# Adding the experts' rows in memory by the scatter, with their gates applied before it

## The reference, cut to what matters

```
logits = xt @ w_router + b_router
top_val, top_idx = lax.top_k(logits, 4)
gate = softmax(top_val)
for each expert e, for the tokens that chose it (rows xb):
    hb = xb @ w_e1[e] + b_e1[e]                 # (1024, 2048)
    y_rows = clamped_swiglu(hb) @ w_e2[e] + b_e2[e]   # (1024, 1024)
y = zeros(T, D).at[row_tok].add(y_rows * row_gate[:, None])
h = layer_norm(DEEPNORM_ALPHA * h + y, ln2_g, ln2_b)
```

## Time and profile before

| | |
|---|---|
| median of 3 runs | 1656.25 us (1654.56 to 1658.57) |
| the profiled execution | 1654.45 us, its span 1652.7 us |
| busy in the span | TensorE 91%, VectorE 29%, ScalarE 15%, POOL 14% |
| chain that ended last | PE 69%, DMA 19% |
| queue q1 (issued by SP) | 445.10 MB, 68.4% of 16 engines' span |
| mean granted clock of TensorE | 0.979 of full |

### The profile page before, as it was taken

The page is one execution under the profiler, slowest core; times in us unless marked ns, Lnnn a source line. Parts: engine busy times, 40 slices in busy tenths (PEclk is TensorE's granted clock), DMA queues, the critical chain, the costliest instruction groups (busy, mean ns, idle before and its releaser), DMA issues.

```text
span 1652.7 us, 30470 instructions
## 1 busy us (share of the span) xinstructions
PE 1498.5 (91%) x12438; PEld 687.6 (42%) x12439; DVE 483.3 (29%) x933; ACT 249.9 (15%) x302; POOL 232.7 (14%) x301
## 2 busy tenths in 40 slices
PE   7999999999999878999997888998799999999955
PEld 6744444444445623344343333333334333344322
DVE  5034343200005634223232223223223222232226
ACT  4011232100001121111110111101011010010112
POOL 1060000000000001211211211211211121111225
PEclk9999999999999889999999999999999999999987
DMA  5523100153304479999999999999999999999945
GB/s 187 181 77 91 30 1 0 48 187 89 89 2 202 153 313 416 413 416 417 415 415 416 415 414 417 416 414 417 415 414 416 417 415 414 387 367 395 411 161 213
DMA packets 136151, 474.31 MB, mean 287 GB/s; under 512 B 16700, under 2 KB 62500, under 8 KB 102840
## 3 DMA queue, kind: packets, MB, share of 16 engines
q1 hardware_dynamic: 123264, 445.10, 68.4%
q0 software_dynamic: 10896, 16.83, 2.8%
q10 hardware_dynamic: 1960, 11.94, 1.8%
HBM read 470.12 MB, written 20.97 MB: 297 GB/s over the span
## 4 chain that ended last, share of the span: by engine, by line
PE 69%; DMA 19%; DVE 3%; issue 3%; SPq 3%; ACT 1%; POOL 1%; ACTq 0%; POOLq 0%; DVEq 0%
PE ps L1417 22%; DMA big<-in_w_e 16%; PE ps L1445 13%; PE ps L1285 7%; PE ps L1206 5%; PE ps L1315 3%; PE ps L1343 3%; PE ps L1299 3%; PE ps L1167 3%; SPq L457 2%; PE ps L1293 2%; DMA rest<-x_rows,idx 2%; PE ps L1234 1%; PE ps L1410 1%; PE ps L1513 1%
## 5 line engine op out<-in xcount | busy, mean ns | idle before, releaser
L1417 PE MATMUL ps<-big,rest 128*32 128x512 f32 x5120 | 571.9, 599 | 70.0 <-DMA big<-in_w_e 36.6
L1417 PEld LDWEIGHTS ps<-big,rest 128*32 128x32 f32 x5120 | 162.0, 111 | 443.2 <-issue 443.1
L1445 PE MATMUL ps<-big,rest 128*32 128x256 f32 x5120 | 287.4, 381 | 19.6 <-DMA big<-in_w_e 16.5
L1445 PEld LDWEIGHTS ps<-big,rest 128*32 128x32 f32 x5120 | 166.8, 110 | 130.8 <-issue 34.9
L1076 DVE TENSOR_TENSOR rest<-ps,rest 128x1024 f32<-128x1024 f32 x32 | 39.2, 1224 | 602.4 <-PE ps L1417 602.4
L736 ACT ACTIVATE rest<-ps 128x1024 f32<-128x1024 f32 x33 | 68.6, 2080 | 459.3 <-PE ps L1410 459.3
L569 POOL DMA_INDIRECT expert_rows<-rest,slot x128 | 127.3, 995 | 59.5 <-issue 32.9
L565 POOL COPY slot<-P 128x4 uint32 x32 | 5.9, 184 | 742.1 <-DVE rest L1095 742.1
L740 ACT ACTIVATE rest<-ps 128x1024 f32<-128x1024 f32 x32 | 32.8, 1024 | 410.1 <-PE ps L1438 410.1
L1206 PE MATMUL ps<-big,rest 128*128 128x512 f32 x192 | 82.8, 592 | 2.8 <-ACT big L612 2.8
L1095 DVE TENSOR_TENSOR rest<-ps,rest 128x1024 f32<-128x1024 f32 x32 | 39.2, 1224 | 132.2 <-PE ps L1445 132.2
(11 more groups left out here) (213 smaller groups left out, 1145.2 us busy)
## 6 DMA issues: line engine op xcount, KB each, us to landing
big<-in_w_e SPq DMA_DIRECT2D x384, 1024.0 KB, 19.8
rest<-in_w_in SPq DMA_DIRECT2D x14, 1024.0 KB, 5.2
big<-expert_rows ACTq DMA_DIRECT2D x4, 2048.0 KB, 15.7
gate_area<-in_w_in SPq DMA_DIRECT2D x8, 512.0 KB, 5.4
rest<-in_w_in SPq DMA_DIRECT2D x8, 512.0 KB, 4.7
big<-in_w_out SPq DMA_DIRECT2D x1, 4096.0 KB, 13.0
X<-in_x SPq DMA_DIRECT2D x4, 512.0 KB, 9.6
gate_area<-in_w_branch_mlstm SPq DMA_DIRECT2D x4, 512.0 KB, 6.4
```

Of the source, the lines that this page charges most:

```text
L1417: last = mm(ps[TB * g:TB * (g + 1), b, :], xT[:, k, b, :], W1[:, k, HW_ * g:HW_ * (g + 1)], start=(k == 0), stop=(k == KD - 1))
L1445: last = mm(ps[TB * g:TB * (g + 1), 4 + b // 2, YW * (b % 2):YW * (b % 2 + 1)], aT[:, b, k % 2, TB * (k // 2):TB * (k // 2 + 1)], W2[:, k ...
```

## The change

- `y_dram`, with a row for each choice, is replaced by `sum_dram`, with a row for each token. Slot numbers become token numbers. The scatter gets `compute_op=ALU.add`: the piece is added to what stands in memory.
- `sum_dram` begins as `DEEP_ALPHA` times the first norm's rows: ScalarE scales `X0` tile by tile and stores it, ahead of the softmax's exponential. POOL waits for these stores (`sum_started`) before its loop.
- The gates are put into the same places as the slots by 16 products, ahead of the second pair of weight rows of the first round, and spread by four, ahead of its last pair. VectorE makes 16 one-hots for them instead of the 16 diagonals, and copies the results out.
- `take_y` gets a second instruction: `yS` times the gates, before `y_ready`.
- At the end four loads of 512 KB bring the sums into `X0`. VectorE takes statistics and subtracts the mean, ScalarE computes the root and multiplies the tile before by it, VectorE adds the bias; the last tile is scaled and biased by VectorE alone. ScalarE's table for logarithm and exponential is loaded ahead of it. TensorE and POOL have nothing left to do there.

```diff
-    y_dram = nc.dram_tensor("expert_rows", (S, TOPK, D), F32, kind="Internal").ap()
-    y_quarters = y_dram.rearrange("t k (g n) -> (t k g) n", g=CG)
+    sum_dram = nc.dram_tensor("sum_rows", (S, D), F32, kind="Internal").ap()
+    sum_quarters = sum_dram.rearrange("t (g n) -> (t g) n", g=CG)
...
                 for b in range(NB):
-                    pool.indirect_dma_start(out=y_quarters, out_offset=bass.IndirectOffsetOnAxis(ap=slot[:, b:b + 1], axis=0),
+                    pool.indirect_dma_start(out=sum_quarters, out_offset=bass.IndirectOffsetOnAxis(ap=slot[:, b:b + 1], axis=0),
                                             in_=yS[:, b, :], in_offset=None,
-                                            bounds_check=S * TOPK * CG - 1, oob_is_err=False).then_inc(y_stored, 16)
+                                            bounds_check=S * CG - 1, oob_is_err=False, compute_op=ALU.add).then_inc(y_stored, 16)
...
             pool.wait_ge(tables_ready, 2)
+            pool.wait_ge(sum_started, 16 * NT)
...
+            act.wait_ge(x1_stored, 16 * NT)
+            for i in range(NT):
+                act.activation(X0v[:, i, :], X0v[:, i, :], ACT.Copy, scale=DEEP_ALPHA).then_inc(x1_scaled, 1)
+                act.wait_ge(x1_scaled, i + 1)
+                act.dma_start(sum_dram[P * i:P * (i + 1), :], X0v[:, i, :]).then_inc(sum_started, 16)
             act.wait_ge(dist_ready, 1)
...
             for i in range(NT):
-                act.dma_start(yg[:, i], y_dram[P * i:P * (i + 1)]).then_inc(yg_landed[i], 16)
+                act.dma_start(X0v[:, i, :], sum_dram[P * i:P * (i + 1), :]).then_inc(sum_landed[i], 16)
+            act.preload_act_table_set("natural_log_exp_and_others")
             for i in range(NT):
-                rstd(NORM2 + i)
+                s0 = 16 * i
+                act.wait_ge(var2_ready, i + 1)
+                step(act.activation(stat[:, s0 + 14:s0 + 15], stat[:, s0 + 13:s0 + 14], ACT.Ln))
+                act.activation(stat[:, s0 + 14:s0 + 15], stat[:, s0 + 14:s0 + 15], ACT.Exp, scale=-0.5).then_inc(rstd2_ready, 1)
+                if i >= 1:
+                    act.wait_ge(centred, i)
+                    act.activation(X0v[:, i - 1, :], X0v[:, i - 1, :], ACT.Copy, scale=stat[:, s0 - 2:s0 - 1]).then_inc(scaled, 1)
...
                 nc.vector.tensor_tensor(yS, ps[:, 4:6, :].rearrange("p a (b n) -> p (a b) n", n=YW),
-                                        b2_all.rearrange("p (a n) -> p a n", a=1).broadcast_to([P, NB, YW]), ALU.add).then_inc(y_ready, 1)
+                                        b2_all.rearrange("p (a n) -> p a n", a=1).broadcast_to([P, NB, YW]), ALU.add).then_inc(y_biased, 1)
+                dve.wait_ge(y_biased, it)
+                gates = gate_table[:, bass.ds(it * NB - NB, NB)].rearrange("p (b a) -> p b a", a=1)
+                nc.vector.tensor_tensor(yS, yS, gates.broadcast_to([P, NB, YW]), ALU.mult).then_inc(y_ready, 1)
...
-                nc.vector.tensor_scalar(gate_diag[:, n, :], ident[:], gw[:, i, k:k + 1], None, ALU.mult).then_inc(diags_ready, 1)
+                nc.vector.tensor_scalar(iter_oh[:, n, :], iota_row, itern[:, n:n + 1], gw[:, i, k:k + 1], ALU.is_equal, ALU.mult).then_inc(gate_oh_ready, 1)
+            dve.wait_ge(gates_done, 1)
+            nc.vector.tensor_copy(gates_f, ps[:, 4, 0:N_ITER]).then_inc(gates_read, 1)
+            dve.wait_ge(gates_spread, 1)
+            nc.vector.tensor_copy(gate_table.rearrange("p (n b) -> p b n", b=NB), ps[:, 5, :].rearrange("p (b n) -> p b n", b=NB)).then_inc(gate_table_ready, 1)
...
+            def gate_products():
+
+                pe.wait_ge(gate_oh_ready, TOPK * NT)
+                for n in range(TOPK * NT):
+                    last = mm(ps[:, 4, 0:N_ITER], place_oh[:, n, :], iter_oh[:, n, :], start=(n == 0), stop=(n == TOPK * NT - 1))
+                last.then_inc(gates_done, 1)
+
+            def gate_copies():
+
+                pe.wait_ge(gates_read, 1)
+                pe.wait_ge(tables_ready, 2)
+                for b in range(NB):
+                    last = mm(ps[:, 5, N_ITER * b:N_ITER * (b + 1)], sv[:, b, :], gates_f, start=True, stop=True)
+                last.then_inc(gates_spread, 1)
...
             for k0 in range(0, KD, 2):
+                if k0 == 2:
+                    gate_products()
+                if k0 == 6:
+                    gate_copies()
                 fc1_rows(1, first_blocks, k0)
```

More of the change, by code:

```diff
@@ L345, in build_program @@
         y_stored = sem("y_stored")
-        yg_landed = [sem(f"yg_landed{i}") for i in range(NT)]
+        sum_landed = [sem(f"sum_landed{i}") for i in range(NT)]
         ln2_landed = sem("ln2_landed")
@@ L581, in _ @@
             scatter(n_it)
-            pool.wait_ge(x1_scaled, 1)
-            pool.wait_ge(diags_ready, TOPK * NT)
-            for i in range(NT):
-                pool.wait_ge(yg_landed[i], 16)
-                row = yg[:, i, TOPK - 1, :]
-                step(nc.gpsimd.tensor_scalar(row, row, gatew[:, TOPK * i + TOPK - 1:TOPK * (i + 1)], None, ALU.mult))
-                nc.gpsimd.tensor_tensor(X0v[:, i, :], X0v[:, i, :], row, ALU.add).then_inc(fourth_added, 1)
         @block.scalar
@@ L1118, in _, with norm_2_statistics @@
             dve.wait_ge(ln2_landed, 32)
-            for i in range(NT):
-                t = X0v[:, i, :]
-                dve.wait_ge(fourth_added, i + 1)
-                for n in range(D // BANK):
-                    dve.wait_ge(combined, 2 * i + n + 1)
-                    half = t[:, BANK * n:BANK * (n + 1)]
-                    nc.vector.tensor_tensor(half, half, ps[:, 2 * (i % 2) + n, :], ALU.add).then_inc(combined_read, 1)
-                    dve.wait_ge(combined_read, 2 * i + n + 1)
-                    piece_statistics(NORM2 + i, n, half)
-                close_statistics(NORM2 + i, D // BANK)
+            def norm_2_statistics(i):
+                t = X0v[:, i, :]
+                s0 = 16 * i
+                dve.wait_ge(sum_landed[i], 16)
+                for n in range(D // BANK):
+                    piece_statistics(NORM2 + i, n, t[:, BANK * n:BANK * (n + 1)])
+                step(nc.vector.bn_aggr(stat[:, s0 + 12:s0 + 14], stat[:, s0:s0 + 12]))
+                nc.vector.tensor_scalar(stat[:, s0 + 13:s0 + 14], stat[:, s0 + 13:s0 + 14], LN_EPS, None, ALU.add).then_inc(var2_ready, 1)
+                layer_norm_center(NORM2 + i, t)
@@ L1129, in _, with norm_2_bias @@
+            def norm_2_bias(i):
+                dve.wait_ge(scaled, i + 1)
+                nc.vector.tensor_tensor(X0v[:, i, :], X0v[:, i, :], bias[:], ALU.add).then_inc(out_ready, 1)
+            for i in range(NT):
+                norm_2_statistics(i)
+                y = norm_2_root(i)
                 if i >= 1:
-                    layer_norm_scale(NORM2 + i - 1, X0v[:, i - 1, :], out_ready)
-                layer_norm_center(NORM2 + i, t)
-            layer_norm_scale(NORM2 + NT - 1, X0v[:, NT - 1, :], out_ready)
+                    norm_2_bias(i - 1)
@@ L1135, in _ @@
+            dve.wait_ge(centred, NT)
+            nc.vector.scalar_tensor_tensor(out=X0v[:, NT - 1, :], in0=X0v[:, NT - 1, :], scalar=y, in1=bias[:],
+                                           op0=ALU.mult, op1=ALU.add).then_inc(out_ready, 1)
         @block.tensor
```

47 lines of the change are left out of this document (26 added, 21 removed).

## The result

The changed kernel takes 1745.19 us (median of 5 runs, 1735.95 to 1750.11), the kernel before 1656.25 us (1654.56 to 1658.57). The ratio is 1.0532, with a 95% interval of 1.0497 to 1.0568. That is 89 us more, where 5 us more was predicted and 1688 us was the upper end. The profiled execution took 1735.95 us, with a span of 1734.2 us; it is the fastest of the five, so its trace shows some 9 us less of the loss than the median has.

A forecast was written before the change was run, and what follows sets the result against it. Weight loading was taken to bound the kernel up to 1277 us, then TensorE's products. First round 5.1, added read 13.3, gather lateness 5.3, minus tail 18.5 gave +5.2 us on 1656.25: 1661.5 us, range 1643 to 1688.

The forecast's parts named there:

- What bounds the kernel before: Expert rounds: weight landings decide up to 1277 us, then TensorE's products, broken twice by gathers of 8.4 us each.
- Tail: After the last bias addition: smaller loads and VectorE alone setting the pace gain 18.5 us (16.5 to 19.5).
- drain: Tail: the accumulating write takes longer to land before the sums can be loaded, 1 us (0 to 3).
- First round: TensorE's 20 extra matmuls placing and spreading the gates delay the first round: +5.1 us (2.5 to 10.4).
- The added read on the DMA engines: Rounds before 1277 us: reading old rows costs one more transfer of the same bytes, +13.3 us (0 to 26.6).
- The gathers' lateness: Last three rounds, after 1277 us: the VectorE product and longer scatters delay gathers, +5.3 us (2.4 to 14.3).
- rival 2: Rounds: accumulating scatters hold up the gather, every two-block round waits: +29.5 us, 1686 us; chance 0.18 including beyond 1675 us.
- The turns on the queue: DMA engines alternate queues packet by packet, so further scatter packets wait for weight packets; cited for the late-gather rival, unsized.

The follow-up runs named there:

- 2.1 us of filling: Kernel before, complete, with POOL memsets of 2304 columns added ahead of each round's four scatters: 1664.88 us, ratio 1.0040.
- the two fillings: Changed kernel with overwriting scatters (no addition), POOL memsets of 2.23 us or 7.0 us ahead of each round's scatters: 1679.29 us and 1775.53 us.

## Why the prediction was wrong, point by point

- **What bounds the kernel before** was read rightly as the weights up to 1277 us, though not from the start: the chain shows its first weight landing at 845.99 us, after some eight rounds. The DMA share of 1.02 and the chain say so the earlier trace rows, and giving back the queue's delay brings the weight waits back. What was not read was how far the next limit stood. That one wait ends last does not say how far behind the next one is: here the gather's was one to two microseconds behind.
- **Tail**: 18.5 us predicted (16.5 to 19.5), 17.7 measured. VectorE's part took 19.1 us (1712.00 to 1731.06) against 20.0. The longer part is the issue: the path from the bias addition to ScalarE's loads grew from 8.55 to 12.25 us (3.7 us; 1.4 us of product, 2.3 us of issues), where 2.2 us had been put down: 1.2 of product and 1.0 of a longer drain. The drain did not come (1.2 us instead of 1.1), and the longer issues, which the prediction left out, came in its place. Right in size, in this part by luck.
- **First round**: +5.1 us predicted. VectorE's first addition on the sums of the first round's first product (line 1088, before 1076) starts at 607.41 us instead of 602.29: +5.1 measured. But one round on, POOL's copy of the slots is already 16.8 us late (676.27 instead of 659.50), and in the kernel without the addition 16.3 to 16.7 us there. Of this 5.1 is the gates' products and 1.4 the product of `take_y`. The other 10 us were in no term of the prediction. In the changed kernel a wait of 4.3 us for a gather is among them (at 662.18 us). The kernel without the addition is as late without such a wait: there TensorE stands three times between 636 and 647 us, for about 2 us each, and comes back at a granted clock of 0.60 (645 to 650 us, 1.00 before). A part is won back later, and 11.4 us remain at about 1400 us. No run separates the causes.
- **The added read on the DMA engines**: 13.3 us predicted (0 to 26.6), and 18.5 us measured in the rounds, out of 23.6 for the addition as a whole. The mechanism was right. Two errors worked against each other: the time of a round was too small, and not each of the 21 rounds counts, since the first eight lost nothing. The term assumed as many bytes again at the rate of the whole, or 0.63 us a round. The queue's share shows 1.16 us a round, 37.2 / 32. The packet count shows why "one more transfer of the same bytes" was too small. The same 16.86 MB moved in 23184 packets instead of 10896, and the 12288 further packets come to 12288 / 2048 = 6 for each scattered row. The runs show the packets and their time together, and not which of the further packets carry the old row. The Trainium skill, "Collectives: The Full Stack", section "The bandwidth ceiling: the fold count and why AG ≠ RS ≠ AR", puts the reducing collective at about half the rate of the copying one, because its add needs two source reads on one ring. It says this of collectives and not of a scatter by indices. Carried over, it gives 0.63 us a round, and the engines' time measured here is 1.8 times that: the trace agrees in direction, and for this indirect scatter the measured number decides.
- **The gathers' lateness**: this is the step that failed. The sentence was "Before 1277 us the wait for weights covers it", and it limited the loss to the last three rounds, +5.3 us (2.4 to 14.3). Measured is 81.6 us, spread over the whole of the experts: 19 gathers in the chain, from 651.87 us on. Two things were wrong in it. The first is the depth of the cover. The weight waits are 2.3 us at most. With 2.1 us of filling most of the delay was still covered, and beyond that the two fillings cost 16 to 20 us for each microsecond. The second is the delay, taken as 1.2 us of product and 1 us of drain. It is 1.4 us of product, 2.3 us of issues and 2.8 us (median) to 6.1 us (the round shown) of landing. The 0.99 us of an issue was taken over from the plain scatter, though the prediction itself names it as what would show rival 2. And when the gather is late by more than the waits for weights, TensorE frees weight rows late, few transfers stand in the queues, and the DMA engines run empty for a part of the time. The loss can then not be made up, and TensorE comes back at the lower clock.
- **Rival 2** had the right mechanism, "every round of two blocks waits", and even its first cause, POOL taking longer to write them. But it priced the delay at three rounds (14.3 us) in contradiction to its own sentence. With the delay of 5.1 us that the trace shows, on top of the product, the two fillings give 35 + (5.1 - 2.2) x 20 = 93 us by itself. It argued with "the same number of issues as before", which is true, and says nothing of their length.
- **The turns on the queue** (the Trainium skill, "DMA: Bandwidth & Descriptors", section "Queues, rings and completion order", a packet at a time between queues): the traces agree as far as they go. Gathers behind the adding scatters land in 10.6 us instead of 7.8. Ahead of them they land in 8.1 us, although the weights' queue takes more of the engines' time there (95.1% instead of 90.2% in 620 to 1290 us), so the gather's own sharing with the weights is not what grew: it is the adding scatters' packets ahead in the same queue. In the tail, without weights, those packets cost no further time. That fits turns taken with the weights' packets, but no run shows the turns themselves.
- **The budget**, by the profiled executions, whose spans differ by 81.5 us. The last bias addition starts 99.2 us later than before (1696.43 instead of 1597.23), and the tail gives back 17.7. Of the 99.2 us, 6.0 are there without the addition and with the gather first (1603.27 us), 20.8 come with the addition (1624.05 us), and 72.4 with the gather behind the scatters. By the medians these steps, tails included, are -16.2, +23.6 and +81.6, together 89 us. The prediction's own terms with their measured sizes, 5.1 - 17.7 + 23.6 + 81.6 = 92.6 us, are not such a sum: the issues in the tail, 2.2 us, stand in both the second and the third.

## What to carry to other kernels

Before a transfer in front of another on the same queue is made longer, price the one behind it: how late it may land before its reader stands, in all rounds and not only in those where it is late already. A wait that "covers" a delay covers it only up to its own length. Beyond that each microsecond of delay counts once in every round that is late: here 16 to 20 us over 32 rounds. Where one queue carries both something that is needed soon (a gather) and something that nobody waits for (a scatter), the first belongs ahead; this was worth nothing in the kernel before and 81.6 us after the change.

## What the runs showed of the hardware

- An indirect scatter that adds takes POOL 1.565 us to issue for 128 rows, and the plain one 0.994 us (128 instructions each, shapes and indices equal).
- The adding scatter goes in more packets: 23184 in the queue instead of 10896 for the same 16.8 MB, six more for each scattered row of 4 KB. Over the whole program the page counts 22957 packets of under 512 bytes with the addition and 16764 without, so about half of the further ones are that small.
- One adding round (256 KB scattered on average) costs the 16 engines 1.16 us more than a plain one (queue share 5.0% instead of 2.8%), more than a transfer of as many bytes at the full rate (0.63 us).
- A gather issued behind four adding scatters landed in 10.6 us (median), behind four plain ones in 7.8 us, and ahead of the adding ones in 8.1 us. Without weight transfers beside them, in the tail, the last adding scatter was waited for 1.2 us beyond its issue, the plain one 1.1 us.
- After a stand of 10 us TensorE's next work was at a lower granted clock, 0.72 in 872 to 880 us, and at 1.00 from 880 us. With 18 such waits in the program the mean of 620 to 1290 us was 0.93 instead of 0.99.
